# A decoder trunk layer on one core: the RWKV chain cut into tiles beneath its column products, and the second norm's token factor applied behind the FFN products

## The reference

```
mixed = cols + (prev - cols) * mu          # cols: 1792 RWKV columns, prev: the token before
r, k, v, wd, ad, gd = split(mixed)         # 512, 512, 512, 64, 64, 128
decay = exp(-exp(-softplus(-(w0 + tanh(wd) @ w2)) - 0.5));  a = sigmoid(a0 + ad @ a2);  g = sigmoid(gd) @ g2
kk = k * k_k / sqrt(sum over the head of (k * k_k)^2);   k = k * (1 + (a - 1) * k_a)
S_t = S * decay + (S @ -kk) (kk * a)^T + v k^T;   y = S_t @ r;   bonus = (sum over the head of r*k*r_k) * v

h2 = x * rsqrt(mean(x^2) + eps) * g2;   x = x + (silu(h2 @ w_gate) * (h2 @ w_up)) @ w_down
```

## Time and profile before

| what | us |
|---|---|
| median of 3 runs (lowest, highest) | 1825.39 (1825.13, 1825.85) |
| the profiled execution | 1821.99 |
| its span | 1820.3 |
| PE busy in it | 1632.3 |
| DVE, ACT, POOL busy | 545.7, 221.0, 87.1 |
| mean granted clock of PE, share of full speed | 0.927 |

### The profile page before, as it was taken

How to read it: one execution, slowest core, us unless ns; L and a number is a source line. 1 busy time by engine, 2 the same in 40 slices (tenths; PEclk the granted TensorE clock), 3 DMA queues, 4 the chain that set the end, 5 groups by cost and what they waited for, 6 DMA issues and landing times.

```text
span 1820.3 us, 26551 instructions
## 1 busy us (share of the span) xinstructions
PE 1632.3 (90%) x11348; PEld 1355.5 (74%) x11348; DVE 545.7 (30%) x900; ACT 221.0 (12%) x475; POOL 87.1 (5%) x160
## 2 busy tenths in 40 slices
PE   4986799998797899999989985999989999999994
PEld 3874699886565787777768874688878888888883
DVE  3227765336457115444310013011120101010002
ACT  1013201012411012222201110000010000000000
POOL 0000000000000002000013230100000000000000
PEclk9997799999898799999987776999989999999997
DMA  3220010111200337111126544332212222222221
GB/s 149 81 71 23 25 36 5 48 41 35 96 24 30 142 126 139 56 53 53 53 87 226 168 149 118 92 102 75 81 49 79 72 79 72 79 69 74 75 73 47
DMA packets 61400, 143.35 MB, mean 79 GB/s; under 512 B 12529, under 2 KB 32066, under 8 KB 59970
## 3 DMA queue, kind: packets, MB, share of 16 engines
q1 hardware_dynamic: 41042, 97.01, 17.3%
q0 software_dynamic: 14480, 42.02, 7.4%
q10 hardware_dynamic: 5760, 2.62, 0.5%
HBM read 134.11 MB, written 11.65 MB: 80 GB/s over the span
## 4 chain that ended last, share of the span: by engine, by line
PE 86%; DVE 10%; ACT 2%; issue 1%; DMA 1%; POOL 0%; DVEq 0%; ACTq 0%; POOLq 0%
PE PS L239 44%; PE PS L1222 6%; PE PS L229 5%; PE PS L1646 4%; PE PS L1236 3%; PE PS L1674 2%; PE PS L1732 2%; PE PS L1381 1%; PE PS L1393 1%; PE PS L255 1%; PE PS L537 1%; PE PS L538 1%; PE PS L525 1%; PE PS L1357 1%; PE PS L990 1%
## 5 line engine op out<-in xcount | busy, mean ns | idle before, releaser
L239 PE MATMUL PS<-xn,ring 128*128 128x260 f32 x2560 | 569.9, 385 | 4.0 <-DVE arena L826 2.5
L239 PEld LDWEIGHTS PS<-xn,ring 128*128 128x128 f32 x2560 | 489.4, 191 | 80.6 <-DVE arena L826 2.9
L239 PE MATMUL PS<-arena,ring 128*128 128x260 f32 x1088 | 242.1, 385 | 3.0 <-DVE arena L1939 1.6
L239 PEld LDWEIGHTS PS<-arena,ring 128*128 128x128 f32 x1088 | 207.6, 191 | 36.0 <-DVE arena L1939 2.0
L1222 PE MATMUL PS<-xn,ring 128*128 128x260 f32 x512 | 120.4, 383 | 0.0
L229 PE MATMUL PS<-xn,ring 128*128 128x260 f32 x416 | 103.5, 402 | 15.0 <-DVE xn L302 13.0
L229 PEld LDWEIGHTS PS<-xn,ring 128*128 128x128 f32 x416 | 80.9, 199 | 32.8 <-DVE xn L302 14.2
L1222 PEld LDWEIGHTS PS<-xn,ring 128*128 128x128 f32 x512 | 94.8, 190 | 13.2
L1646 PE MATMUL PS<-arena 128*128 128x256 f32 x256 | 72.2, 451 | 2.4 <-DVE arena L1788 2.4
L1646 PEld LDWEIGHTS PS<-arena 128*128 128x128 f32 x256 | 58.6, 232 | 14.0 <-DVE arena L1788 2.9
L1996 DVE TENSOR_TENSOR arena<-PS,arena 128x520 f32<-128x520 f32 x22 | 15.4, 700 | 150.7 <-ACT arena L1988 150.7
(11 more groups left out here) (420 smaller groups left out, 1810.5 us busy)
## 6 DMA issues: line engine op xcount, KB each, us to landing
ring<-in_w SPq DMA_DIRECT2D x133, 512.0 KB, 3.5
arena<-in_pages SPq DMA_DIRECT2D x64, 192.0 KB, 3.7
arena<-in_pages POOLq DMA_DIRECT2D x64, 192.0 KB, 3.9
ring<-in_w SPq DMA_DIRECT2D x24, 256.0 KB, 3.2
arena<-in_x POOLq DMA_DIRECT2D x2, 2080.0 KB, 8.2
o_winp<-in_win POOLq DMA_DIRECT2D x8, 511.0 KB, 19.9
arena<-in_pages_v SPq DMA_DIRECT2D x48, 64.0 KB, 1.9
ring<-in_w SPq DMA_DIRECT2D x8, 384.0 KB, 3.1
```

The source lines that it names most:

```text
L239: ins = nc.tensor.matmul(PS[:, 2 * bank + half, 0:HALF], weight(g, k), src[:, k0 + k, half * HALF:(half + 1) * HALF], start=first and k == ...
```

## The change

It has these parts, which are made together:

- The RWKV columns are made in the order decay and a, gate, k, r, v (`COL_ORDER`; the host reorders the weight). They use two bank pairs; the other two serve lora, head sums and the samples' sums.
- `raw` shrinks to two slots. ACT's copy of column idx waits for mix idx-2, PE's column idx for the copy of idx-2. Each mix also copies the last prompt token and the 8 samples (9 elements) to a small buffer `SHO`, from which the shift output is sent after the last mix.
- The chain is cut by tile and put between columns in all three lists: lora after columns 2 to 5 (the gate's four only after the rows), key squares after each key's mix, head sums two tiles at a time behind columns 6 and 7, the norms by tile, the scans after mix 6, the exponentials on ACT behind columns 9 and 10, the samples' `s_sa` behind column 11, the bonus behind columns 12 and 13, then the rows. ACT evicts 10 of 12 row pairs, DVE two. The exponentials are taken in place in the operand of the chunk products, and each hat is one instruction. The state is loaded once `cum_prev` and `ws` are done, into the buffer of the log decay.
- The last doubling level leaves out the product of the transposed inverse (538) and its two additions, whose result isn't read; POOL and PE no longer wait for them.
- In `Merge`, ACT writes x2 times the norm's gain to XN tile by tile. PE runs the first gate and up tiles on that, and the sum of squares behind them. DVE applies 1/root to gate and up as it reads them from PSUM (two operations), then multiplies twice; ACT's sigmoid reads the scaled gate.
- The barriers behind `merge` and `ffn` go.

The core of the diff:

```diff
+                column(1)
+                column(2)
+                lora(0)
+                lora(1)
+                column(3)
...
+                column(6)
+                kk_sums(0)
+                kk_sums(1)
+                column(7)
+                kk_sums(2)
+                kk_sums(3)
+                column(8)
+                column(9)
+                column(10)
+                column(11)
                 pe.wait_ge(*at("s_sa_terms"))
+                for t in (2, 3):
+                    pe.wait_ge(*at("kk_max", t))
...
+                column(12)
+                bonus_sums(0)
+                bonus_sums(1)
+                column(13)
+                bonus_sums(2)
+                bonus_sums(3)
...
+                for r in range(8):
+                    row(r)
...
+                for r in range(9, 12):
+                    row(r)
+                pe.wait_ge(*at("s_v_used"))
+                for j in range(8, 12):
+                    lora(j)
...
+                pe.wait_ge(*at("s_y_out"))
+                row(8)
                 pe.wait_ge(*at("hats"))
```

DVE's list, and the two waits of a column:

```diff
+                def raw_evac(idx):
+                    act.wait_ge(*at("tile", start["rwkv"] + idx))
+                    if idx >= 2:
+                        act.wait_ge(*at("mixed", idx - 2))
...
+                mix(6)
                 v.wait_ge(*at("lw"))
                 for t in range(4):
                     nc.vector.tensor_tensor_scan(CUM[:, t, :], C("reset"), LW[:, t, 0:T], 0.0, ALU.mult, ALU.add).then_inc(*step("dve", "cum"))
...
+                mix(7)
+                key_max(0)
+                key_max(1)
...
+                mix(8)
+                key_max(2)
+                key_max(3)
+                key_norm(0)
+                mix(9)
+                key_norm(1)
+                key_norm(2)
+                key_norm(3)
...
+                mix(10)
+                v.wait_ge(*at("s_rwkv"))
...
+                mix(11)
...
+                mix(12)
+                mix(13)
```

The FFN:

```diff
+                for k in range(KT):
+                    act.wait_ge(*at("x2", k))
+                    nc.scalar.activation(XN[:, k, :], X2[:, k, :], ACT.Copy, scale=col("g2", k)).then_inc(*step("act", "x2_gain", k))
...
+                for k in range(KT):
+                    pe.wait_ge(*at("x2_gain", k))
...
+                    part(pe, start["up"], 0, range(k, k + 1))
+                pe.wait_ge(*at("x2", 6))
+                product(pe, start["up"] + 1, 2, XN)
+                pe.wait_ge(*at("x2", 7))
                 norm_pe(pe, "norm2", SQ2t)
...
+                    pe.wait_ge(*(at("x2", 5) if i == 1 else at("gate_scaled", i - 2)))
                     product(pe, g, i % 2, XN)
+                    pe.wait_ge(*(at("norm2", "mean") if i == 1 else at("up_scaled", i - 2)))
...
+                    nc.vector.tensor_tensor(halves(GF[i % 2]), pair(i % 2), halves(rs[:, :]), ALU.mult).then_inc(*step("dve", "gate_scaled", i))
...
+                    nc.vector.tensor_tensor(halves(H[:, i, :]), pair(2 + i % 2), halves(rs[:, :]), ALU.mult).then_inc(*step("dve", "up_scaled", i))
```

More of the change, by code:

```diff
@@ L354, in build @@
         MX = tiles(mixed, 14)
-        RC = tiles(raw, 14)
+        RC = raw[:, 6176:6176 + 2 * (TOK + 1)].rearrange("p (s n) -> p s n", s=2)
+        SHO = small_r[:, 176:302].rearrange("p (t n) -> p t n", t=14)
         shift = small_r[:, 0:112].rearrange("p (t b) -> p t b", t=14)
@@ L373, in build @@
         OFF = MB[:, :, :, 0, :].rearrange("p c t n -> p (c t) n")
-        Ssr, SAr, SBr = rows[:, 0:2048], rows[:, 2048:4096], rows[:, 4096:6144]
+        Ssr, SAr, SBr = LWr[:, 0:2048], rows[:, 0:2048], KKr[:, 0:2048]
+        COL_ORDER = (12, 13, 4, 5, 6, 7, 0, 1, 2, 3, 8, 9, 10, 11)
         def sview(ap):
@@ L427, in pe, with lora @@
             def pe(pe):
[L428 to L441, removed]
+                def lora(j):
                     kind, t = j // 4, j % 4
                     if j == 0:
-                        pe.wait_ge(*at("kk_max"))
-                    if j >= 4:
-                        pe.wait_ge(*at("lora_out", j - 4))
+                        pe.wait_ge(*at("lora"))
+                        pe.wait_ge(*at("tanh"))
+                    if j == 8:
+                        pe.wait_ge(*at("siggd"))
+                    if 2 <= j < 8 or j >= 10:
+                        pe.wait_ge(*at("lora_out", j - 2))
                     rows_ = (slice(0, 64), slice(64, 128), slice(0, 128))[kind]
@@ new lines, in bonus_sums, with column @@
+                def bonus_sums(t):
+                    pe.wait_ge(*at("bonus_terms", t))
+                    pe.wait_ge(*(at("s_sa_used") if t < 2 else at("bonus_out", t - 2)))
+                    head_sums("bonus_sums", t)
+                def column(idx):
+                    if idx >= 2:
+                        pe.wait_ge(*at("raw", idx - 2))
+                    product(pe, start["rwkv"] + idx, idx % 2, XN)
+                column(1)
+                column(2)
+                lora(0)
+                lora(1)
@@ new lines, in pe @@
+                column(3)
+                lora(2)
+                lora(3)
+                column(4)
+                lora(4)
+                lora(5)
+                column(5)
+                lora(6)
+                lora(7)
+                column(6)
[8 more added lines that the diff above has]
+                column(11)
@@ L473, in pe @@
                 ins.then_inc(*step("pe", "s_y"))
[L475 to L489, removed]
+                pe.wait_ge(*at("s_y_out"))
+                row(8)
                 pe.wait_ge(*at("hats"))
-                pe.wait_ge(*at("row", 10))
-                pe.wait_ge(*at("row", 11))
+                for r in range(8, 12):
+                    pe.wait_ge(*at("row", r))
+                for j in range(8, 12):
+                    pe.wait_ge(*at("lora_out", j))
                 for c in range(NC_):
@@ L607, in act @@
[L607 to L615, removed]
@@ L628, in act @@
[L628 to L637, removed]
+                nc.scalar.activation(AR[:, :, :, 0, :], AR[:, :, :, 0, :], ACT.Exp).then_inc(*step("act", "e_prev"))
```

307 lines of the change are left out of this document (196 added, 111 removed).

## The result

The changed kernel takes 1778.07 us in the median of four runs (1775.61 to 1780.53), the kernel before in the same comparison 1825.26 (1824.17 to 1825.85): a ratio of 0.9742, 95% interval 0.9725 to 0.9759. Forecast were 1777, with 1767 to 1788. The profiled execution took 1778.72 with a span of 1776.6.

The account below looks back on a forecast made before the run. A DVE chain with PE waiting at each link, an idle DVE beneath the columns, and the second norm were to give time; the rest is PE at full clock. -37.3 + 2.0 - 3.5 - 11.4 + 1.4 = -48.8: 1777 us, range 1767 to 1788.

Parts of the forecast that it names:

- rival 4: RWKV columns 9 to 11 wait for the DVE chain through the two raw slots; 21 us more, 1798; 3%.
- First chunk product, -37.3: RWKV chain put beneath the columns: first chunk product at 188.2 us, before at 225.47; -37.3 us.
- Hats: Two hats in DVE's stretch, each one strided instruction: 4.9 us together, with +4 kept for the range.
- Chunk products, +2.0: Clock falls at the chunk products, behind the one-column products: +2.0 us (0 to +4).
- Last level, -3.5: Last doubling level drops 128 passes on PE and two DVE additions: -3.5 us (-2 to -3.7).
- Norm -11.4: Second norm: first FFN tile runs right behind the last `out` product; -11.4 us (-9 to -11.7).
- FFN end +1.4: Two more DVE operations between last FFN tile and down products, where one stood: +1.4 us (to +3).
- rival 1: Clock falls after the 3.3 and 2.9 us gaps, stays low through one-column products; adds 25 us, 1802; 8%.
- Rival 3: Smaller gap before key sum 2, more DVE overlap, clock holds at chunk products: -4.5 us, 1772; 8%.
- rival 5: Slower: PE never regains high clock after the 3.3 us gap; -48.8 + 57 = +8, 1833; 3%.
- Rival 2: RWKV state's load starves until DVE stops at 136.5; everything behind shifts by 5.3 us, 1782; 8%.
- The base: Difference set against the timed median, 1825.39 us, giving 1777; against the profiled execution, 1821.99, 1773.

Follow-up runs that it names:

- e5: Changed kernel with two extra 128x2048 multiplications in VectorE's unbroken stretch, ahead of bk_hat; 1784.53 us.
- e6: Changed kernel with sixteen extra 128x512 products (32 passes) on TensorE ahead of its wait for the SA terms; 1780.37 us.
- e7: Changed kernel with the two hat multiplications moved from before s_sa_used to behind mix 12; 1773.77 us.
- e13: Changed kernel with five unused 128x252 products in the 3.06 us wait and three in the wait ahead of the y square sums; 1777.46 us.
- e2: Kernel before with the RWKV part and the shorter last doubling level, merge and FFN as before; 1790.22 us, ratio 0.9806.
- e3: Kernel before with the last doubling level alone cut short; 1821.13 us, ratio 0.9980.
- e4: Changed kernel with the first two key maxima ahead of the subtraction and mix 7 in DVE's list; 1773.69 us.
- e10: Changed kernel with eleven unused 128x252 products on TensorE before its 3.06 us wait for the third key maximum; 1778.17 us.
- e1: Kernel before with the norm-factor part alone, the two barriers left out; 1813.6 us, ratio 0.9938.
- e11: Changed kernel with nine unused 128x252 products in the second half of the wait ahead of the y square sums; 1780.12 us.
- e9: Changed kernel's instructions reordered to remove waits before the first chunk product and in the FFN; 1761.13 us, ratio 0.9646 to the kernel before.

## Why the prediction was right, and where it wasn't

- **The mechanism** was as forecast: PE's longest wait 9.29 (10.4) for the SA terms, DVE unbroken for 44.85 (46.5), PE the path behind `s_sa_used`; e5, e6 and e7 show it. No column waited for a raw eviction (rival 4), no wait for the scaled gate.
- **First chunk product, -37.3:** the term that was mis-sized, -33.3. By the walk: mix 8 at 111.64, not 108.2 (+3.4); DVE's stretch -1.6; PE from `s_sa_used` on 35.5, not 33.4 (+2.1). Of the +3.4, 1.5 is the changing between columns and lora tiles: I had 7.02 and 1.76 a round, 8.78, and the chain that ended last in the changed kernel's profile has rounds of 9.16 (62.92, 72.08), four of them.

```profile
62.92 7.21 PE PS L239 x32
72.08 7.21 PE PS L239 x32
```

 Some 1.7 is the clock behind the 3.06 wait, which I had bounded by 0 to +2 and taken at 0; e13 measured it. The other 0.2 is the start of column 1. Of the +2.1 behind `s_sa_used`, 0.8 is its last step: I had 2.1 for copy, pair 8 and eviction, all at full clock, and it took 2.9, since the clock had fallen behind the one-column products and pair 8 took 1.79 us (0.95 for a pair in the row at 167.34). The rest is small groups, each a little longer than its share of a column: lora 8 to 11 3.8 (3.5), one-column products 3.9 (3.5), value sums 3.6 (3.45).
- **Hats:** 2.29 each, as a plain instruction of that size; the bound of +4 was not needed.
- **Chunk products, +2.0:** measured +2.1, the clock at 0.50 in their first 4 us, as forecast (1.00 from 225 to 229 us before). The fall came earlier than this term had it, as pair 8 shows.
- **Last level, -3.5:** it was -4.0, a little beyond the bound of -3.7. From the last start of the first products in the doubling to the y sums it is 102.4 us before and 98.5 in the changed kernel, in e2 and in e3 alike; e3's median has -4.3. The -3.5 in the table is a coincidence: the same step holds 0.3 less in the levels ahead and 0.7 more in the y square sums.
- **The y square sums** aren't in the sum. They took 6.17 (5.46 before), and behind the next gap the clock was 0.75 from 396 to 400 us, where it had been 1.00 from 432 to 436 before: the products there took 43.8 us for 42.35, which is more than the 1.2 lost from the variance to the last `out` tile. e4, e6, e7 and e10, whose code is the same there, took 42.35, so this loss isn't shown to come from the change.
- **Norm -11.4, FFN end +1.4:** -11.6 and +1.4, so -10.2; e1, which has both, -11.9 in the medians, with an interval of -14.8 to -7.8.
- **Rivals 1, 3 and 5:** the clock fell behind the wait of 3.06, not behind that of 2.61, and was back within one column (1.7 us, not the 25 of rival 1 or the 57 of rival 5). Rival 3 had the clock hold at the chunk products, and there it was 0.50.
- **Rival 2:** the state's load stood behind `ws`, was issued at 120.73 and landed 5.0 us later, 13 ahead of L842 at 138.96. The Trainium skill, "SBUF — State Buffer", section "Who interferes with whom", has a DVE instruction in a two-port mode and POOL shut each other out for the length of an instruction, and says that `tensor_tensor` has no such mode. Beside this load DVE ran two reciprocals with one `tensor_tensor` between them, without a pause, and the load took what it took before; whether a reciprocal runs in such a mode no run here shows, so that this is no test of the rule. Nor do the prediction's two rows test it: the earlier load (issued at 161.26) lay beside 1.7 us of one-input multiplications, but then beside 2.3 of a two-input one. The shift's output, 9.9 before, took 1.9; it now reads one run of 126 numbers per partition, where it read 14 pieces of nine, and no run tells this from what DVE does beside it.

```profile
arena<-in_rwkv_state POOLq DMA_DIRECT2D x1, 1024.0 KB, 5.0
...
o_shift<-arena POOLq DMA_DIRECT2D x1, 63.0 KB, 1.9
```

- **The base:** the median was hit within 1.1 us because two errors met: the sum was 5 too large against the profiles, and the profiled execution of before lay 3.3 under its median. Against that execution the forecast would have been 1773, and 5 off. That the total came out so close is luck; the terms above are what was right. The lower end of the range, 1773 - 5, should have been 1768.

## What to carry to other kernels

Walk each engine's queue in the new order with the durations of the old trace: it gave the place of every wait, and the list of waits that were left gave the next version, 17 us faster. Price groups that alternate by the rhythm they have when they alternate, and where several short waits on TensorE follow each other, count a fall of its clock among them even if none alone caused one before; here filling waits with useless products gained nothing measurable, and taking the waits away paid. Compare profiles stretch by stretch and from a common start: one long stretch of the same code took from 835.7 to 842.2 us, a spread larger than what most of the edits here are worth. Say against which execution a difference is set: here the profile and the median of the same kernel lay 3.3 us apart, as much as a whole part of the change.

## What the runs showed of the hardware

- The length of a wait alone didn't tell whether the clock falls. In the wait for `s_sa_used` it held behind 2.49 (e2), 2.61, 2.77 (e10), 2.87 (e11) and 2.92 (e6), where the head sums took 2.00; it fell behind 1.97 (e13, 3.54) and 3.21 (e4, 2.65). Behind the same wait of 2.49 after the variance, products of the same code took 42.35 us in ten profiles and 43.8 to 44.0 in four. Behind the wait of 3.06 the key sums took 2.65 to 3.67 in six profiles.

```profile
156.34 2.00 PE L450 MATMUL PS<-arena,cn 128*128 128x260 f32 x8 [2.92 <-DVE arena L863]
```

- The 128 one-column products ran at 0.50 behind a wait of 6.00 (6.99). Reached at full clock they ran at 1.00 in 3.90 in the changed kernel, and the clock fell right behind them. In e9 it fell during them, though PE had been busy without a gap since 131 us: 1.00 to 168 us and 0.50 from there, 5.35 for the 128.

```profile
165.97 5.35 PE L545 MATMUL PS<-arena 64*64 64x1 f32 x128
```

- The doubling levels, the same code at a clock of 1.00 throughout, took from 48.5 to 50.6 us from the first to the last start of their first product (48.9 before, 48.6 after, 50.6 in e4, 50.3 in e6, 50.2 in e9). PE issued fewer passes in the same time (us, PE busy, clock, DMA share, GB/s), first in the changed kernel, then in e4; what delays them isn't shown.

```profile
253.00:263.00 10.00, 10.00 (x352) 1.00 0.02 5
```

```profile
260.00:270.00 10.00, 9.83 (x320) 1.00 0.02 5
```
